# A convolution and mixture-of-experts block on one core: rounded bias and banks first, two more places for gates, the general path behind the fourth group

## What is computed

```python
a, gate = jnp.split(x @ pw1_w + pw1_b, 2, axis=-1)        # 272 x 2048 @ 2048 x 4096
u = a * jax.nn.sigmoid(gate)
u = conv(u, dw_w, 31 taps, depthwise, causal) + dw_b
u = jax.nn.silu(layer_norm(u, ln_g, ln_b))
mix = u @ pw2_w + pw2_b                                   # 2048 x 2048
h = layer_norm(DEEPNORM_ALPHA * h + mix, ln_mix_g, ln_mix_b)
# grouped top-2 of 32 experts for each token, weights normalised
ffn = sum over the two experts e of: weight * ((silu(h @ w_gate[e]) * (h @ w_up[e])) @ w_down[e])
h = layer_norm(DEEPNORM_ALPHA * h + ffn, ln_ffn_g, ln_ffn_b)
```

## Time and profile before

| | us |
|---|---|
| median of three runs | 1324.66 (1323.47 to 1326.42) |
| the profiled execution | 1324.57 |
| its span, first to last instruction | 1322.4 |
| mean granted clock of TensorE | 0.972 of full speed |
| PE busy | 1222.5 (92% of the span) |
| DVE, ACT, POOL busy | 434.9, 262.1, 272.6 |
| read from memory | 462 MB, 351 GB/s over the span |

### The profile page before, as it was taken

How to read it: one execution, slowest core, us unless ns; L and a number is a source line. 1 busy time by engine, 2 the same in 40 slices (tenths; PEclk the granted TensorE clock), 3 DMA queues, 4 the chain that set the end, 5 groups by cost and what they waited for, 6 DMA issues and landing times.

```text
span 1322.4 us, 15650 instructions
## 1 busy us (share of the span) xinstructions
PE 1222.5 (92%) x6125; PEld 646.8 (49%) x6125; DVE 434.9 (33%) x881; ACT 262.1 (20%) x351; POOL 272.6 (21%) x110
## 2 busy tenths in 40 slices
PE   7999998999798999899899989989998998979895
PEld 7999996587443343243234334323432432343332
DVE  2899998601920221203021220202121121202026
ACT  4665555432310010010001001000100100010001
POOL 5999989187200000000000000000000000000001
PEclk8999998899899999999999989999999999999998
DMA  9766555155679999999999999999999999999993
GB/s 285 214 187 184 165 160 230 61 191 185 260 292 429 428 428 427 427 428 428 429 428 428 428 429 428 428 428 429 428 429 428 428 429 428 428 427 384 424 414 144
DMA packets 102953, 464.73 MB, mean 351 GB/s; under 512 B 4353, under 2 KB 71937, under 8 KB 75265
## 3 DMA queue, kind: packets, MB, share of 16 engines
q1 hardware_dynamic: 102914, 464.20, 87.1%
HBM read 462.09 MB, written 2.10 MB: 351 GB/s over the span
## 4 chain that ended last, share of the span: by engine, by line
PE 55%; DMA 34%; DVE 3%; POOL 3%; issue 2%; SPq 1%; ACT 1%; DVEq 0%; ACTq 0%; POOLq 0%
DMA ring<-in_wu 33%; PE ps L1374 23%; PE ps L1126 12%; PE ps L1231 6%; PE ps L1425 5%; PE ps L1295 4%; POOL ring_r L466 3%; PE ps L1312 2%; DMA xT<-in_xT 1%; SPq L401 1%; PE ps L1171 1%; PE ps L1333 1%; PE ps L1346 1%; PE ps L1164 0%; DVE terms_r L886 0%
## 5 line engine op out<-in xcount | busy, mean ns | idle before, releaser
L1374 PE MATMUL ps<-ring,gain_bias 128*64 128x512 f32 x2048 | 462.4, 606 | 51.8 <-DMA ring<-in_wu 43.7
L1374 PEld LDWEIGHTS ps<-ring,gain_bias 128*64 128x64 f32 x2048 | 158.4, 139 | 349.6 <-issue 349.2
L466 POOL TENSOR_TENSOR ring_r<-ring,ring_r 128x2048 fp32r<-128x2048 f32 x47 | 216.6, 4622 | 62.7 <-ACT ring_r L545 62.7
L1425 PE MATMUL ps<-ring,xT 128*64 128x512 f32 x992 | 219.7, 595 | 4.7 <-DVE xT L1023 4.7
L501 POOL TENSOR_TENSOR rstd<-mv,minus_half 128x1 f32<-128x1 f32 (+1 forms) x3 | 1.8, 600 | 973.9 <-DVE mv L1082 960.8
L1018 DVE TENSOR_TENSOR xT<-xT,ps 128x256 f32<-128x256 f32 x32 | 13.5, 422 | 463.9 <-ACT xT L666 463.9
L771 DVE SCALAR_TENSOR_TENSOR ps<-u,par,ps 128x256 f32<-128x256 f32 x400 | 159.5, 483 | 5.9 <-ACT ps L592 5.9
L1126 PE MATMUL ps<-x_hi,ring_r 128*128 128x272 f32 x1024 | 136.0, 290 | 3.7 <-ACT x_hi L552 3.7
L1425 PEld LDWEIGHTS ps<-ring,xT 128*64 128x64 f32 x992 | 68.5, 137 | 142.6 <-issue 135.3
L1126 PEld LDWEIGHTS ps<-x_hi,ring_r 128*128 128x128 f32 x1024 | 132.3, 190 | 3.9 <-ACT x_hi L552 3.9
L1312 PE MATMUL ps<-xT,pickT 128*128 128x512 f32 x240 | 115.2, 612 | 0.0
(11 more groups left out here) (171 smaller groups left out, 678.4 us busy)
## 6 DMA issues: line engine op xcount, KB each, us to landing
ring<-in_wg SPq DMA_DIRECT2D x62, 2048.0 KB, 15.7
ring<-in_wu SPq DMA_DIRECT2D x62, 2048.0 KB, 20.2
ring<-in_wd SPq DMA_DIRECT2D x62, 2048.0 KB, 16.7
ring<-in_w SPq DMA_DIRECT2D x48, 1024.0 KB, 6.0
ring<-in_wg SPq DMA_DIRECT2D x4, 1024.0 KB, 5.9
ring<-in_wu SPq DMA_DIRECT2D x4, 1024.0 KB, 9.1
ring<-in_wd SPq DMA_DIRECT2D x4, 1024.0 KB, 15.3
xT<-in_xT SPq DMA_DIRECT2D x2, 1088.0 KB, 10.2
```

The source lines that it names most:

```text
L466: nc.gpsimd.tensor_tensor(ring_r[:, lo_slot(c), :], ring[:, raw_slot(c), :], ring_r[:, hi_slot(c), :].bitcast(f32), ALU.subtract).then_inc ...
L1374: mm = nc.tensor.matmul(ps_gu[hh * SLOTS:(hh + 1) * SLOTS, :].rearrange("p (a f) -> p a f", a=2), xgT[:, 4 * m + c, q, :], ring[:, s:s + 3 ...
L1425: mm = nc.tensor.matmul(ps_y[g * SLOTS:(g + 1) * SLOTS, nb, :], midT[:, f % 2, (f // 2) * SLOTS:(f // 2 + 1) * SLOTS], ring[:, s, g * 1024 ...
```

## The change

Three edits come together. First, b2 is rounded into a high and a low part of float32r (on ACT and DVE, by columns, then brought by two transfers into two rows), and `prime_bias` multiplies two rows of ones by them. POOL shifts tiles 0 to 7 before it makes the low part of chunk 34 (`W1_CHUNKS + 2`). The parts of the squares change their order, the banks are begun among the squares in another order, and banks 4 and 5 before the second product, behind two matmuls whose result is written over. Second, the ring gets two more places, 12 and 13, over the place of `xT`; y, act_sb, mid and midT move elsewhere. The first gate transfer of odd experts goes there, so that the first gate transfer of an expert waits for m = 1 of the expert two before (`first_used`); in odd experts gate and up change sides in places 4 to 7 and in `ps_gu`. Third, the loop over the groups ends after group 3, the general path stands behind it, and a second loop does groups 4 to 6 (`late + i`). Left out of the diff below are new semaphores and unused lines around it.

```diff
--- before.py
+++ after.py
+MID_QUAD = 4
...
-SQUARED = ((0, 4), (4, 8), (8, 12), (12, 14), (14, 15), (15, 16))
+SHIFTED = ((0, 4), (4, 8), (8, 12), (12, 14))
+SQUARED = ((0, 4), (4, 8), (14, 15), (8, 12), (12, 14), (15, 16))
...
-        ring_r = under("ring_r", [P, RING, 2048])
-        ring = sb("ring", [P, RING, 2048])
-        xT_r = under("xT_r", [P, KT, LEN])
+        with nc.sbuf_tensor("ring_r", [P, RING, 2048], f32r) as ring_r, \
+                nc.sbuf_tensor("xT_r", [P, KT, LEN], f32r) as xT_r:
+            pass
+        ring_xT = sb("ring", [P, RING * 2048 + KT * LEN])
+        ring = ring_xT[:, 0:(RING + 2) * 2048].rearrange("p (s n) -> p s n", n=2048)
...
-        xT = sb("xT", [P, KT, LEN])
+        xT = ring_xT[:, RING * 2048:RING * 2048 + KT * LEN].rearrange("p (k t) -> p k t", t=LEN)
...
+        gain_bias_r = under("gain_bias_r", [P, 2, D])
+        b2_rows = gain_bias_r[0:2, 1, :]
...
-        b2_row = bias[0:1, :]
+        b2_cols = sb("b2_cols", [P, KT])
+        b2_parts = sb("b2_parts", [P, 2, KT], f32r)
+        ones_r = sb("ones_r", [2, P], f32r)
...
-        expert_sb = xT[:, :, :].rearrange("p k t -> p (k t)")
-        y = expert_sb[:, 0:D]
-        act_sb, mid = expert_sb[:, D:D + 256], expert_sb[:, D + 256:D + 512]
-        midT = expert_sb[:, D + 512:D + 768].rearrange("p (c s) -> p c s", c=2)
+        y_all = sb("y", [P, D])
+        y = y_all[:, :]
+        act_sb, mid = u[:, 0, 0:256], u[:, 1, 0:256]
+        midT = par[:, 0:256].rearrange("p (c s) -> p c s", c=2)
...
+        def load_late(eng):
+
+            return eng.value_load(quads_i[0:1, 3:4], min_val=MID_QUAD, max_val=(BLOCKS - 1) * QUADS + MID_QUAD)
...
-            sp.dma_start(b2_row, b2).then_inc(b2_s, 16)
+            sp.dma_start(b2_cols[:, :], b2.rearrange("o (p k) -> (o p) k", k=KT)).then_inc(b2_s, 16)
             with sp.Fori(1, KT // 4) as i:
                 pw1_chunks(i)
+            sp.wait_ge(b2_lo, 1)
+            for part in range(2):
+                sp.dma_start(b2_rows[part:part + 1, :].bitcast(f32).rearrange("o (p k) -> o p k", k=KT),
+                             b2_parts[:, part, :].bitcast(f32)).then_inc(b2_rows_s, 16)
             for k in range(RAW):
...
+                    if a == 1 and kind != "down" and q % 2 == 1:
+                        s = {"gate": 6, "up": 4}[kind]
                     w_v = {"gate": wg_v, "up": wu_v, "down": wd_v}[kind]
                     src = w_v[ds(e, 1), a, :, :].rearrange("o p n -> (o p) n")
+                    if (kind, a) == ("gate", 0) and not n_is_first(n):
+                        odd = q % 2
+                        sp.wait_ge(first_used, n)
+                        s = RING if odd else 0
+                        sp.dma_start(ring[:, s:s + 2, :].rearrange("p a n -> p (a n)"), src
+                                     ).then_inc(arrived_odd if odd else arrived[0], 16)
+                        continue
                     if in_halves(n) and kind != "down":
                         for half in range(2):
-                            sp.wait_ge(freed[4 * a + 2 + half], n)
+                            if (a, half) == (0, 1):
+                                sp.wait_ge(first_used, n + 1)
+                            else:
+                                sp.wait_ge(freed[4 * a + 2 + half], n)
                             sp.dma_start(ring[:, s + half, :], src[:, half * 2048:(half + 1) * 2048]
                                          ).then_inc(arrived[s + half], 16)
...
+                    elif (kind, a) == ("up", 0):
+                        sp.wait_ge(first_used, n + 1)
...
-            with sp.Fori(1, QUADS - 1) as i:
+            with sp.Fori(1, MID_QUAD) as i:
                 quad(i)
             with sp.If(quads > QUADS):
-                with sp.Fori(QUADS - 1, last) as i:
+                with sp.Fori(MID_QUAD, late) as i:
                     quad(i)
+            with sp.Fori(0, QUADS - 1 - MID_QUAD) as i:
+                quad(late + i)
...
             with pool.Fori(0, KT // 4 - 1) as i:
                 low_pass(i)
             low_pass(KT // 4 - 1, tiles=3)
-            low(W1_CHUNKS + 2, 2)
-            shift_tiles(0, 4)
+            for a, b in SHIFTED[:2]:
+                shift_tiles(a, b)
             pool_sum(KT - 1, 3)
-            for a, b in SQUARED[1:4]:
+            for a, b in SHIFTED[2:]:
                 shift_tiles(a, b)
-            for n in range(W1_CHUNKS + 3, W_CHUNKS):
+            for n in range(W1_CHUNKS + 2, W_CHUNKS):
...
+            act.wait_ge(consts, N_CONSTS)
+            nc.scalar.activation(ones_r[:, :], ones[0:2, :], ACT.Copy)
+            act.wait_ge(b2_s, 16)
+            nc.scalar.activation(b2_parts[:, 0, :], b2_cols[:, :], ACT.Copy).then_inc(b2_hi, 1)
...
             for c, (a, b) in enumerate(SQUARED):
-                if c < 4:
-                    act.wait_ge(centred, c + 1)
+                if (a, b) in SHIFTED:
+                    act.wait_ge(centred, SHIFTED.index((a, b)) + 1)
                 else:
-                    act.wait_ge(taps, a * TILE_OPS + DVE_TAPS + (3 if c == 4 else 2))
+                    act.wait_ge(taps, a * TILE_OPS + DVE_TAPS + (3 if a < KT - 1 else 2))
                 nc.scalar.activation(squares[:, a:b, :], conv[:, a:b, :], ACT.Square).then_inc(squared, 1)
-                if c == 0:
+                if c == 2:
...
-                    nc.scalar.activation(act_sb, ps_gu[:, 0:256], ACT.Silu).then_inc(act_done, 1)
+                    nc.scalar.activation(act_sb, ps_gu[:, q % 2 * 256:q % 2 * 256 + 256], ACT.Silu).then_inc(act_done, 1)
...
+                if tile == 4:
+                    dve.wait_ge(b2_hi, 1)
+                    nc.vector.tensor_tensor(b2_parts[:, 1, :], b2_cols[:, :], b2_parts[:, 0, :].bitcast(f32),
+                                            ALU.subtract).then_inc(b2_lo, 1)
...
+            done(nc.vector.tensor_scalar(quads_f[:, 3:4], quads_f[:, 0:1], float(MID_QUAD - QUADS), None, ALU.add))
+            done(nc.vector.tensor_scalar(quads_f[:, 4:5], quads_f[:, 3:4], 16.0, -8.0, ALU.mult, ALU.add))
...
-                nc.tensor.matmul(ps[:, bank, :], ones[0:1, :], b2_row[:, bank % 4 * 512:(bank % 4 + 1) * 512],
+                nc.tensor.matmul(ps[:, bank, :], ones_r[:, :], b2_rows[:, bank % 4 * 512:(bank % 4 + 1) * 512],
...
             pe.wait_ge(made, KT - 1)
             pe.wait_ge(taps, SHIFT_TILES * TILE_OPS)
             nc.tensor.matmul(ps_shift, mean_w[:, :], total_c, start=True, stop=True).then_inc(shift_ps, 1)
-            pe.wait_ge(b2_s, 16)
-            for bank in (0, 1):
-                prime_bias(bank)
+            pe.wait_ge(b2_rows_s, 32)
             pe.wait_ge(made, KT)
-            for bank in (2, 3):
-                prime_bias(bank)
             squares_part(0)
             pe.wait_ge(x_s, 16)
             for bank in (0, 1):
+                prime_bias(bank)
                 prime_x(bank)
             squares_part(1)
             for bank in (2, 3):
+                prime_bias(bank)
                 prime_x(bank)
-            squares_part(2)
             pe.wait_ge(shifted, 1)
             mean_part(KT - 2)
-            squares_part(3)
-            squares_part(4)
+            for c in range(2, 5):
+                squares_part(c)
             mean_part(KT - 1).then_inc(sums, 1)
             squares_part(5).then_inc(sums, 1)
             for bank in (6, 7):
                 prime_bias(bank)
                 prime_x(bank)
-
-            def prime_rest():
-
-                pe.wait_ge(var_in, 1)
-                for bank in (4, 5):
-                    prime_bias(bank)
-                    mm = prime_x(bank)
-                mm.then_inc(primed, 1)
+            pe.wait_ge(var_in, 1)
+            for _ in range(2):
+                nc.tensor.matmul(ps[:, 4, :], ident_alpha[:, :], h[:, 0, 0:512], start=True, stop=True)
+            for bank in (4, 5):
+                prime_bias(bank)
+                mm = prime_x(bank)
+            mm.then_inc(primed, 1)
...
-                if step_k == PW2_LEAD - 1:
-                    prime_rest()
...
-            keep_clock(4)
+            keep_clock(4).then_inc(first_used, 1)
...
+                        odd = g == 0 and q % 2 == 1
+                        pair_of = slice(s + 2, RING + s + 1, RING - 2) if odd else slice(s, s + 3, 2)
...
-                            landed(4 * g, n)
+                            if odd:
+                                pe.wait_ge(arrived_odd, 16 * (2 * i + q // 2) + 16)
+                            else:
+                                landed(4 * g, n if g == 1 else 2 * i + q // 2)
...
-                                    ring[:, s:s + 3:2, c * FF + hh * 256:c * FF + (hh + 1) * 256],
+                                    ring[:, pair_of, c * FF + hh * 256:c * FF + (hh + 1) * 256],
...
-                        if half == 1 or n_is_first(n):
+                        if m == 1:
+                            mm.then_inc(first_used, 1)
```

(9 more changed lines are left out.)

51 lines of the change are left out of this document (35 added, 16 removed).

## The result

The changed kernel takes 1320.62 us (median of 9 runs, 1319.17 to 1323.23); the kernel before, timed beside it, 1325.06 (9 runs, 1322.41 to 1330.24). The ratio is 0.9962, 95% interval 0.9952 to 0.9972: 4.4 us faster by the medians, 5.0 by the ratio. The forecast was 1315.0 and its range ended at 1319.8. The sign was right; about half of the 9.6 us came. The profiled execution of the changed kernel took 1322.32 us (span 1320.5), 1.7 above its median, so its marks are read beside a second profile of each kernel (experiments 9 and 10).

A forecast was written before the change was run, and what follows sets the result against it. The prediction took the time before the weights stream without a break, and any DMA standstill after, as the bound; 1324.57 - 6.4 (convolution) - 0.8 (places) - 2.4 (jump) = 1315.0 us, range 1310.5 to 1319.8.

The forecast's parts named there:

- Part 1: Convolution: rounded bias and reordered banks start the second product sooner; 6.4 us gained, bounds 4.4 and 8.5.
- PE's list from there to the mean: TensorE's work from first squares to the mean: the old 12.8 us plus 1.0 for four rounded biases.
- Rival (c): Convolution: mean no earlier, the second product's start held by x or the clock; 1317.0 us, chance 0.15.
- The rounded bias: Convolution, TensorE: one instruction per rounded bias, taken as 0.25 us, 1.0 us for four.
- the room for chunk 36: Before step 2 of the second product: chunk 36's low part has room; TensorE waits 2 us for GpSimd once.
- The costs set to nothing: Rounding beside the first product, delayed low parts (chunks 38, 39 by 12 and 1 us), two router steps: no cost.
- Part 2: Two more ring places: expert 1's gate transfer goes without waiting for TensorE; 0.8 us gained, bounds 0 and 4.9.
- Rival (f): Odd experts: operands read ten slots apart slow matmuls; at half speed 57 us slower, 1382; chance 0.03.
- Part 3: Jump over the general path moves from expert 28 to 16: 4.7 us saved less 2.3 lost, 2.4 us gained.
- rival (a): End of expert loop: leaving it costs, not the jump; expert 28 loses 2.3 us again, 1317.3; chance 0.10.
- rival (b): Jump at expert 16: the new place hides nothing, 4.7 us only moves to the middle; 1317.4, chance 0.12.
- my count of dry stretches: Weight stream around the stall at expert 28: 3.4 us without data, where arrivals showed 4.7.

The follow-up runs named there:

- experiments 9 and 10: Second profiles, nothing altered, of the changed kernel (1321.19 us) and of the kernel before (1325.69 us).
- e3: Changed kernel with the exact bias back for all banks, no rounding, banks 0 to 3 before the squares; 1314.29 us, ratio 0.9920.
- e4: Changed kernel with 18 unused small matmuls filling TensorE's stand before the first squares; 1315.01 us, ratio 0.9933.
- e8: Changed kernel with only the four rounded biases of banks 0 to 3 moved ahead of the first squares; 1317.34 us, ratio 0.9941.
- e1: Kernel before with the first edit alone (rounded bias, order of shifts, squares and banks); 1323.59 us, ratio 0.9988.
- e11: Second profile of the changed kernel with the exact bias back (e3), nothing else altered; 1312.62 us.
- e5: Kernel before with the second edit alone (two more ring places for gate transfers); 1321.35 us, ratio 0.9967.
- e6: Kernel before with the third edit alone (general path behind the fourth group); 1319.22 us, ratio 0.9956.
- e7: Kernel before without the never-taken conditional loop for more than eight groups; 1320.77 us, ratio 0.9965.

## Why the prediction was wrong

**What bounds the kernel: right.** All marks after *first* move with it, and the order of transfers, chain and dents was as read.

**Part 1: the step that failed.** "PE's list from there to the mean is the old 230.88-218.09 = 12.8 us plus four rounded biases." The old list held the clock's recovery at 221; I carried that duration over with the list, though the change altered both what the list stands behind and what is in it. The 3.70 us of exact bias between the first product and the squares are gone and TensorE stands there 4.35 us, not 3.80, and four two-row products stand among the squares. The words "PE having stood before them as now" hide it. Which of the two kept the clock down until 228.0 is open; that the low clock took the gain is shown by e3, e4 and e8. The list took 234.74-215.05 = 19.7 us instead of 13.8. With the clock kept (e4) it took 228.35-213.93 = 14.4. Rival (c) named the clock, with 0.15, but priced it as the mean coming no earlier; it came 3.9 us *later*, which the bounds (4.4 gained at the least) didn't allow for either. Of 6.4 us there was 1.0 in the first profiles, 0.7 in the second and 1.6 by the timed runs of e1.

The rounded bias was sized 0.25; at 2.4 GHz it takes 229.69-229.26 = 0.43, at 1.2 GHz 0.72. That is 0.7 us in four, a small share. The start of the squares, x, the room for chunk 36 and the carrying of the gain to the statistics held nearly, as e4 shows: 5.2 to 5.8 against 6.4, with one wait for GpSimd of 2.23 us. That e4's mean (228.35) meets the forecast's 228.8 is in part luck, since its first product ended 1.1 us earlier. The costs set to nothing (roundings, delayed low parts, router steps) show nothing in e4's sum either.

**The first expert.** Not forecast: 1.4 us of cold gather. It fell on both profiles of the changed kernel and neither of before, but e3 and e11 show that it isn't the change's own.

**Part 2: right, a little small.** Forecast 0.8. *First* to the landing of expert 15 takes 441.1 and 441.0 after, 442.0 before; e5 has 441.2, e6 441.9, e7 442.4. So 0.7 to 1.5 us between the pairs; the 443.5 of before again holds a late transfer (the landings of experts 5 and 6 lie 30.9 us apart). Rival (f) is refuted by the 607 ns.

**Part 3: right kind, sizes off.** The dent moved and came out as two short ones, no exit costs anything (rival (a) is refuted by TensorE's rows at expert 28 and by e7), and the place hides part of it (rival (b) is refuted by e5). Two sizes failed. "What it does to the end is read better from arrivals ... 4.7 us late" took in the 1.5 that are lost without any jump too; the jump's own price was 3.1 to 3.8, nearer to the 3.4 that my count of dry stretches gave and that I scaled away from. And at expert 16 2.0 and 1.8 of it are left (444.1 and 443.9 less 442.1). So 445.2 - 444.1 = 1.1 to 445.9 - 443.9 = 2.0, not 2.4. What I hadn't thought of at all is that the stall's length changes with the build. Had it come out at 3 us, part 3 would have given all of the 3.1 to 3.8.

The traces bear the Trainium skill (Runtime: NRT & Kernel Launch, "Instruction fetch mechanics") out in one point: a taken branch to code that isn't held stalls the engine until that code is fetched. At the jump there are one or two transfers of instructions, and without the jump (e7) there is no stall. The prediction read the same rule as asking for a stall at each way back of the loop, too. The window that the Trainium skill states there, two pages of 256 instructions, would ask for it, since a group's body is 494 matmuls and 492 weight loads. The same section of the Trainium skill gives TensorE room for 2048 instructions. The trace of before agrees with the second figure and not with the first: no transfer of queue 8 from 590 to 1180, and no gap of TensorE at a way back.

**The sum, from the two profiles of each kernel (means):** convolution 0.8 gained, gather 1.4 lost, *first* to 15 1.7 gained (0.95 of it part 2, 0.75 half of the late transfer that one profile of before holds), jump 1.6 gained, end 0.3 gained: 3.0, which is the difference of the mean spans, 1322.95 and 1319.95. The medians differ by 4.4; 1.4 us of that no profile shows, and stays unassigned.

## What to carry to other kernels

Work moved out of an engine's idle stretch is not always a gain. A duration that was measured behind a wait holds for the clock that it was measured at, so ask what TensorE does *while it waits* and what else changes in the list before carrying it over, and look at the granted clock afterwards. Filler in the gap, or the slower form left there, costs nothing; here the exact bias in the gap beats the rounded one among the squares by 4.3 to 4.8 us in the convolution. And compare a stall at a jump between builds, and count the transfers of instructions in it, before taking its length for a property of the algorithm.
